# A hybrid attention and linear-attention block on one core: PSUM banks dealt out anew, half of one step's probabilities left in 32 bits, and who stores the linear-attention outputs

## The reference, cut to what matters

```
def blocked_attention(q, k, v):            # 8 query heads, 2 key/value heads, head size 64
    s = einsum('bqhgd,bkhd->bhgqk', q * Dh ** -0.5, k)      # latent: 2048 + 256 keys
    p = softmax(s, axis=-1)
    return einsum('bhgqk,bkhd->bqhgd', p, v)

def gla_chunked(q, k, v, g, s0):           # 4 heads, chunks of 64 tokens, forwards and backwards
    a = where(tril, einsum('bnihd,bnjhd->bnhij', q_t, k_t), 0)
    o_intra = einsum('bnhij,bnjhv->bnihv', a, v)
    o_inter = einsum('bnihd,bnhdv->bnihv', q_t, s_prev)
    ...
o_gla = rms_norm(o_f + o_b[:, ::-1], gla_g) * silu(og)
out = concatenate([o_gla, o_att], axis=-1) @ w_out
```

## Time and profile before

| | |
|---|---|
| median of three runs | 3334.68 us |
| the profiled execution | 3334.31 us |
| its span in the profile | 3332.5 us |
| PE busy, weight loads busy | 95%, 83% |
| DVE, ACT, POOL busy | 71%, 51%, 52% |
| attention | about 256 to 1064 us |
| GLA outputs | about 1488 to 1607 us |

### The profile page before, as it was taken

How to read it: one execution, slowest core, us unless ns; L and a number is a source line. 1 busy time by engine, 2 the same in 40 slices (tenths; PEclk the granted TensorE clock), 3 DMA queues, 4 the chain that set the end, 5 groups by cost and what they waited for, 6 DMA issues and landing times. The chain is left out here.

```text
span 3332.5 us, 48435 instructions
## 1 busy us (share of the span) xinstructions
PE 3163.3 (95%) x18066; PEld 2767.8 (83%) x18066; DVE 2377.7 (71%) x3263; ACT 1712.5 (51%) x2475; POOL 1718.4 (52%) x918
## 2 busy tenths in 40 slices
PE   6999999999997999998899799999999999999998
PEld 5986777777775997878688699999999999788886
DVE  4888999999996774349533688889888887223367
ACT  5867888888887784211344444443443333211122
POOL 2658999999997111101023377767766774000001
PEclk8999999999998999999999899999999999999999
DMA  6432101111111344338566577757785775554576
GB/s 223 163 122 79 49 22 50 45 51 45 47 33 58 135 150 134 113 117 259 168 214 196 168 243 231 239 161 227 228 257 155 222 220 158 213 188 178 180 262 220
DMA packets 434297, 518.42 MB, mean 156 GB/s; under 512 B 39712, under 2 KB 325328, under 8 KB 434064
## 3 DMA queue, kind: packets, MB, share of 16 engines
q1 hardware_dynamic: 387600, 414.46, 39.1%
q10 hardware_dynamic: 43440, 91.07, 7.9%
q0 software_dynamic: 3024, 9.80, 0.7%
HBM read 341.62 MB, written 173.64 MB: 155 GB/s over the span
## 5 line engine op out<-in xcount | busy, mean ns | idle before, releaser
L867 POOL TENSOR_TENSOR att_tlo<-att_prob,att_thi 128x1024 fp32r<-128x1024 f32 x292 | 694.3, 2403 | 41.7 <-ACT att_thi L1024 40.9
L168 PE MATMUL fu_p<-fu_hhi,fu_whi 128*128 128x384 f32 x1848 | 620.2, 336 | 24.9 <-PEq L113 17.3
L170 PE MATMUL fu_p<-fu_hhi,fu_wlo 128*128 128x384 f32 x1848 | 619.1, 335 | 0.0
L169 PE MATMUL fu_p<-fu_hlo,fu_whi 128*128 128x384 f32 x1848 | 619.1, 335 | 0.0
L1019 ACT ACTIVATE att_prob<-att_p_s 128x512 f32<-128x512 f32 x584 | 340.2, 591 | 88.4 <-PE att_p_s L919 81.2
L168 PEld LDWEIGHTS fu_p<-fu_hhi,fu_whi 128*128 128x128 f32 x1848 | 348.2, 188 | 27.3 <-issue 17.7
L1051 DVE TENSOR_REDUCE att_mx<-att_p_r 128x1 f32<-128x512 f32 x496 | 331.0, 684 | 33.4 <-PE att_p_r L882 32.3
L169 PEld LDWEIGHTS fu_p<-fu_hlo,fu_whi 128*128 128x128 f32 x1848 | 348.4, 189 | 0.0
L170 PEld LDWEIGHTS fu_p<-fu_hhi,fu_wlo 128*128 128x128 f32 x1848 | 348.2, 188 | 0.0
L1024 ACT ACTIVATE att_thi<-att_prob 128x1024 fp32r<-128x1024 f32 x292 | 309.7, 1061 | 9.3
L1866 POOL TENSOR_TENSOR fu_wsum<-fu_ws 128x1024 f32<-128x1024 f32 x66 | 182.7, 2768 | 237.0 <-DMA fu_ws<-in_w_ffn_dram 174.7
(11 more groups left out here) (371 smaller groups left out, 8027.4 us busy)
## 6 DMA issues: line engine op xcount, KB each, us to landing
fu_ws<-in_w_ffn_dram SPq DMA_DIRECT2D x132, 512.0 KB, 8.4
gated_d<-fu_out SPq DMA_DIRECT2D x99, 448.0 KB, 5.9
fd_src<-gated_d SPq DMA_DIRECT2D x63, 704.0 KB, 4.1
second_d<-fu_hs ACTq DMA_DIRECT2D x77, 512.0 KB, 3.3
fu_hs<-in_w_ffn_dram ACTq DMA_DIRECT2D x121, 256.0 KB, 4.3
fd_second<-second_d SPq DMA_DIRECT2D x40, 512.0 KB, 5.8
fd_w<-second_d SPq DMA_DIRECT2D x37, 512.0 KB, 5.3
ga_h<-hT_d SPq DMA_DIRECT2D x36, 512.0 KB, 4.2
```

What stands on the lines that cost most here:

```text
L168: pe.matmul(out, ah, bh, start=first, stop=False)
L169: pe.matmul(out, ah, bl, start=False, stop=False)
L170: return pe.matmul(out, al, bh, start=False, stop=last)
L867: pool.tensor_tensor(tlo[:, sl, :], prob[:, sl, :], thi[:, sl, :].bitcast(F32), ALU.subtract).then_inc(s.lo, 1)
```

## The change

Four things change.

1. **Banks.** `p_r` has three banks, `p_o` one. An item now waits for the item three places earlier. The first values of a unit wait until DVE has read the unit before (`osum` of that unit, not of the one before it). To give this time, PE's order changes around the end of a unit: the last values (both halves) come early in their step, and the first values of the next unit come at the end of the next step.
2. **Modulation parameters.** Their half chunk goes into a `p_r` bank as an item of the ring; DVE adds the bias at the start of the next step.
3. **One half-step unsplit.** For the second half of step 6 of each latent unit ACT copies no `thi` and POOL makes no `tlo`; PE multiplies the values with `prob` itself, as 32-bit floats (fp32), in one matmul in place of two in fp32r.
4. **GLA outputs.** ACT stores the finished tile itself, after its copy. SP loads the keys first, and waits for them only until the keys' buffer is free (`af`, `abk`), then the queries. In the output projection ACT waits once for these stores.

```diff
+    EXACT = (6,)
-        p_r = [ph.ps("p_r0"), ph.ps("p_r1")]
+        p_r = [ph.ps(f"p_r{i}") for i in range(3)]
-        p_o = [ph.ps("p_o0"), ph.ps("p_o1")]
+        p_o = ph.ps("p_o")
+        def exact(b, j, i):
+            return b.nds > 1 and i == 1 and j in EXACT
+        def split_cols(b, j):
+            return slice(0, ROW if exact(b, j, 1) else 2 * ROW)
...
+                if chunk is not None and j == CHUNK_STEP:
+                    S.part = (chunk, self.item(s.mod, chunk[0] * 2 + (chunk[1] + 1)))
...
+                        cols = split_cols(e, j)
-                        pool.tensor_tensor(tlo[:, sl, :], prob[:, sl, :], thi[:, sl, :].bitcast(F32), ALU.subtract).then_inc(s.lo, 1)
+                        pool.tensor_tensor(tlo[:, sl, cols], prob[:, sl, cols], thi[:, sl, cols].bitcast(F32), ALU.subtract).then_inc(s.lo, 1)
...
-                                wait(pe, s.osum, b.n - 1)
+                                wait(pe, s.osum, b.n)
+                        if exact(b, j, i):
+                            last = pe.matmul(p_o[:, :], v.bitcast(F32), prob[:, sl, cols], start=False, stop=j == b.nds - 1)
...
+                    begins = S.val and S.val[1] == 0
+                    ends = S.val and not begins and S.val[1] == S.val[0].nds - 1
-                    if S.val:
+                    if S.val and not begins:
                         values(0)
+                    if ends:
+                        values(1)
                     if pieces:
                         piece(*pieces.pop(0))
                     if S.now:
                         scores(1)
+                    if begins:
+                        for p in pieces:
+                            piece(*p)
+                        values(0)
+                        values(1)
...
-            if T := U.at(5):
-                sp.wait_ge(s.et, t + 1)
-                sp.dma_start(g.mix_tile(tile_at(t))[:, 0:GH * P], mT[:, par, :]).then_inc(s.st[par], 16)
+                wait(sp, s.af, GH * (t - OUT_BUFS + 1))
+                wait(sp, s.abk, GH * (t - OUT_BUFS + 1))
+                sp.dma_start(kT[:, n], ...).then_inc(s.qk[n], 16)
                 wait(sp, s.o, t - OUT_BUFS + 1)
                 ...two loads of qp...
-                sp.dma_start(kT[:, n], ...).then_inc(s.qk[n], 16)
...
                 act.activation(mT[:, par, :], p_m[:, :], ACT.Copy).then_inc(s.et, 1)
+                act.wait_ge(s.et, t + 1)
+                act.dma_start(g.mix_tile(tile_at(t))[:, 0:GH * P], mT[:, par, :]).then_inc(s.st[par], 16)
```

More of the change, by code:

```diff
@@ L751, in __init__ @@
             def __init__(self):
-                self.chunk, self.slots, self.ahead = None, [None] * SLOTS_P, iter([])
-                self.index, self.fin, self.ready, self.out, self.store, self.summed, self.done, self.ring = 1, None, None, None, None, None, [None, None, None], [None, None]
+                self.chunk, self.part, self.slots, self.ahead = None, None, [None] * SLOTS_P, iter([])
+                self.index, self.fin, self.ready, self.out, self.store, self.summed, self.done, self.ring = 1, None, None, None, None, None, [None, None, None], [None] * len(p_r)
             def item(self, sem, count):
-                bank, before = self.index % 2, self.ring[0]
+                bank, before = self.index % len(p_r), self.ring[0]
                 self.index += 1
-                self.ring = [self.ring[1], (sem, count)]
+                self.ring = self.ring[1:] + [(sem, count)]
                 return p_r[bank], before
@@ L792, in unit_steps @@
                     n = AHEAD if last else (PLAN if e.n else PLAN_FIRST)[j]
-                    S = self.step(e, j, v, n, v is not None and last, load if j == 0 else None)
-                    S.chunk = chunk
+                    S = self.step(e, j, v, n, v is not None and last, load if j == 0 else None, chunk)
                     yield S
@@ L931, in values @@
                         cols = slice(i * ROW, (i + 1) * ROW)
-                        pe.matmul(p_o[b.par][:, :], v, thi[:, sl, cols], start=j == 0 and i == 0, stop=False)
-                        last = pe.matmul(p_o[b.par][:, :], v, tlo[:, sl, cols], start=False, stop=j == b.nds - 1 and i == 1)
+                        if exact(b, j, i):
+                            last = pe.matmul(p_o[:, :], v.bitcast(F32), prob[:, sl, cols], start=False, stop=j == b.nds - 1)
+                        else:
+                            pe.matmul(p_o[:, :], v, thi[:, sl, cols], start=j == 0 and i == 0, stop=False)
+                            last = pe.matmul(p_o[:, :], v, tlo[:, sl, cols], start=False, stop=j == b.nds - 1 and i == 1)
                         if i == 1:
@@ L960, in step @@
                         scores(1)
-                    if len(pieces) > 1:
-                        piece(*pieces.pop(0))
-                    if S.val:
+                    if begins:
+                        for p in pieces:
+                            piece(*p)
+                        values(0)
                         values(1)
-                    for p in pieces:
-                        piece(*p)
-                    if S.chunk is not None and S.now[1] == CHUNK_STEP:
-                        (e, j), (c, half) = S.now, S.chunk
-                        wait(pe, s.osum, e.n)
+                    else:
+                        if len(pieces) > 1:
+                            piece(*pieces.pop(0))
+                        if S.val and not ends:
+                            values(1)
+                        for p in pieces:
+                            piece(*p)
+                    if S.part is not None:
+                        (c, half), (bank, before) = S.part
+                        if before:
+                            pe.wait_ge(*before)
                         pe.wait_ge(s.aw, c * 16 + 16)
@@ L975, in step @@
                                 col = half * HALF + q * QUART
[L976 removed]
+                                last = pe.matmul(bank[q * COLS:(q + 1) * COLS, 0:QUART], cpad[:, k, :], aw[:, k, col:col + QUART],
                                                  start=k == 0, stop=k == KC - 1)
@@ L1080, in step @@
                 def step(S):
+                    if S.sent is not None:
+                        (c, half), (bank, _) = S.sent
+                        dve.wait_ge(s.chunk, c * 2 + (half + 1))
+                        dve.wait_ge(s.adab, c * 32 + 32)
+                        dve.tensor_tensor(mod[:, half, :], bank[:, 0:QUART], adab[:, half, :], ALU.add).then_inc(s.mod, 1)
                     for p in S.early:
@@ L1111, in step @@
                         piece(*p)
-                    if S.chunk is not None and S.now[1] == CHUNK_STEP + 1:
-                        e, (c, half) = S.now[0], S.chunk
-                        dve.wait_ge(s.chunk, c * 2 + (half + 1))
-                        dve.wait_ge(s.adab, c * 32 + 32)
-                        dve.tensor_tensor(mod[:, half, :], p_o[1 - e.par][:, 0:QUART], adab[:, half, :], ALU.add).then_inc(s.mod, 1)
                 schedule(step)
@@ L2041, in step @@
                             act.wait_ge(s.table, 1)
+                            for n in range(2):
+                                act.wait_ge(g.op_st[n], 16 * (NT // 2))
                         act.wait_ge(s.tr, t + 1)
```

21 lines of the change are left out of this document (11 added, 10 removed).

## The result

The changed kernel takes **3362.56 us** (median of four runs, 3355.16 to 3365.59), the kernel before, on the same chip, 3334.70. The ratio is 1.0076 (95% interval 1.0062 to 1.0089): slower, as forecast, by 28 us where 12 were forecast. The time stands 1.6 us above the upper end of the range. The profiled execution took 3361.18 us, its span is 3359.4.

The account below looks back on a forecast made before the run. PE was taken to set attention's pace, POOL close behind, and DVE that of the GLA outputs. 3334.31 + 15 (attention) - 2.2 (GLA outputs) = 3347 us, slower; range for 8 in 10: 3318 to 3361.

Parts of the forecast that it names:

- the ring is late again: Rival, attention: ring costs 0.5 us per unit more and four context units stall twice; 3368 us, chance 0.10.
- PE sets the pace: Attention: PE, busy 789 of 808 us, is the limit; POOL, at 772, is close behind.
- Three ring banks: Attention's maxima ring: 1.4 us per unit lost in waits becomes about 0.2 (bounds 0 and 0.7).
- One output bank: Attention, unit's end: PE waits 1.14 us for `osum` plus 0.10 restart, 1.24 per unit (bounds 0.6 and 1.6).
- There is no slack elsewhere: Attention: nothing else in PE's unit absorbs the 1.24 us stall for the single output bank.
- Half a step in fp32: Latent units: one 0.88 us fp32 matmul replaces two 0.233 slots, +0.41 per unit on PE; POOL's relief buys nothing.
- Modulation in the ring: Units with a half chunk: same 1.1 us on PE, its bank free; zero, within 0.1.
- the walk: Attention: following DVE beside PE through the steps, PE finds its ring bank free by 0.3 to 1.3 us.
- Sum for attention: Units without a chunk 24.35 against 23.98, with one 25.35 against 24.78; 32 x 0.46 = +15 us.
- Context units at nothing: Attention's context units: no added cost, as ACT reads their values out before PE ends the next step's list.
- GLA outputs: GLA outputs: earlier query loads remove PE's load waits, -2.2 us (bounds 0 and -4); DVE's 5.85 per tile stays.
- The rival "the terms cancel": Attention: stall near 0.85, no other wait left, +0.07 to +0.16 per unit; 3336 us, chance 0.15.

Follow-up runs that it names:

- Run 3: Kernel before with the unsplit fp32 half step alone, banks and order as before: 3347.32 us, ratio 1.0031.
- run 6: Changed kernel with ACT's copy of the outputs (`osb`) moved one step earlier, ahead of the second exponential and `thi`: 3315.14 us, ratio 0.9931.
- run 10: Run 6 with two ring banks for the maxima instead of three: 3349.20 us, ratio 1.0038.
- run 7: Run 6 without the unsplit half step, all steps split in two rounded pieces: 3317.48 us, ratio 0.9938.
- Run 8: Changed kernel with the last maxima piece before a unit's first values computed five times, filling the wait for `osum`: 3347.08 us, ratio 1.0027.
- run 4: Changed kernel with two ring banks for the maxima instead of three, the eighth bank idle: 3407.62 us, ratio 1.0209.
- run 5: Run 4 with four matmuls into the idle bank ahead of each unit's first values: 3412.09 us, ratio 1.0228.
- run 2: Changed kernel without the unsplit fp32 half step, all steps split in two rounded pieces: 3334.06 us, ratio 0.9994.
- run 9: Changed kernel with one scores matmul more per unit, far from the wait for `osum`: 3366.51 us, ratio 1.0087.

## Why the prediction was right, and what it missed

The direction was forecast rightly and for the right reason; the size was not: 28 us came where 12 were forecast. The time alone is nearer to the rival "the ring is late again" (3368) than to the forecast (3347), but that mechanism did not occur: PE's weight loads wait 7.6 us for reductions, where it was 40.3 before. Step by step, in the prediction's order:

- **PE sets the pace.** Right. POOL waits 103.8 us for `thi`. By weight loads (600 of 808 us in the kernel before) POOL (772) would be the fuller engine. The Trainium skill's rule in "Perfetto Trace Analysis", Identifying the Most-Contended Engine, judges TensorE by FLOP utilization or by weight-load time, and by the second it would point to POOL; the first was not worked out here. Run 3 contradicts the second: 1.18 us less for POOL and 0.40 more for PE cost 0.39 a unit.
- **Three ring banks, -1.2 a unit.** 1.15 and 0.93, measured in runs 6 and 10 where nothing else differs.
- **One output bank, +1.24 a unit.** The wait is 1.09 and the loss 1.26 in the trace. Taking it away gives 24.25 - 23.03 = 1.22 in units without a chunk, but only 0.63 in those with one (25.45 - 24.82). "There is no slack elsewhere" was thus right for one kind of unit. The Trainium skill asks in "Perfetto Trace Analysis", Optimizing Tensor Performance, for matmul groups that rotate through PSUM banks; runs 6 and 10 say where that pays here: a third bank for the ring is worth some 35 us, while one output bank causes no wait in the middle of the stage once its read-out starts early.
- **Half a step in fp32, +0.41.** 0.39 to 0.40, in two pairs of kernels. Four times the 128-column row was a good scale. That the fp32 step buys nothing was right, and stays right without the stall (run 7).
- **Modulation in the ring, no wait.** Mis-sized: a chunk makes a unit 1.20 longer, forecast 1.00. The weight loads of L1000 wait 6.5 us for reductions, 16 times, so the bank was not free as the walk had it.
- **Sum for attention.** Units that keep the clock: 24.25 and 25.45, forecast 24.35 and 25.35. The two errors of 0.10 cancel, which is luck: 16 x (0.27 + 0.67) = 15.0 us, forecast 15. The forecast also took all 32 units for such units. Only 26 distances are; they give 12.1 us, and the first two and the tail give 0.8 back. So without the falls the stage grows by 11.3 us from the first `qb` copy to the last, not by 15. Run 8, where the clock is kept, confirms the smaller sum: +8.9 us by its ratio, where 12.5 were forecast (11.3, and 2.5 at the end of the stage, less 5 in the GLA outputs, is 8.8). That its time of 3347.08 is the forecast's 3347 is chance, since the kernel before took 3338.23 in its group.
- **Context units at nothing.** Their last wait of 2.1 us and the fall behind it cost about 2.5 us.
- **GLA outputs, -2.2.** Mis-sized: -5.3, known within about 3. The direction and the two waits in the middle were right; the last four tiles give 3 us more.
- **What is missing: TensorE's clock.** The prediction valued a wait of 1.1 us at its length. In 11 of 31 cases it also left the matmuls behind it at half speed, 17 us in the latent units alone, more than the 11 us of all the rest. Nothing in the rows read before spoke of it: the ring's waits were short (0.17 us in the earlier trace rows, 0.34 on average in the earlier trace rows), and the clock stood at 1.00 in the pair of units. This term alone carried the time past the range, which had been made from the stall's and the fp32 matmul's bounds.
- **The rival "the terms cancel".** Its sum is off. With 0.85 for the stall and no other wait, a unit without a chunk is 22.9 + 0.85 = 23.75, 0.23 less than before, and only the one with a chunk is longer (0.07 to 0.17). That gives some 3330, not 3336; both count as "same".

On the cause: it is shown that the falls stand behind the waits for `osum` or, in runs 4 and 5, with the ring's wait at the same place; that they go when the wait is filled with matmuls (run 8) or removed (run 6); that the fp32 matmul is not needed (run 2); and that equal units with equal waits fall or don't (run 9). Because one equal wait in several has a fall, the absence of falls in one kernel could be chance. Over the changed kernel and runs 2 and 9, 19 of 81 waits of 1.09 us have one behind them (nine, one and nine); of the 27 filled waits of run 8 none has, and in the middle of run 6's stage there is neither a wait for `osum` nor a fall. From run 9 it follows that the moment plays a part. In the changed kernel a fall lengthens the pair of units from 49.70 to 51.23 us, and the nine falls ahead of the tail come 51.2 us apart; that the pair's new length keeps them in step is my reading, and no run varied it on its own. Why the falls of run 2 stopped after the first is open in the same way.

The two profiles add up: span +26.9 us; first `qb` copy +2.3 (ahead of attention, where the program is the same; over all the traces here this copy starts between 254.4 and 257.3 us, so it belongs to the execution and not to the change); to the last copy +28.3, of which 17 are the falls; then about +2.5 at the very end of attention, where the 2.1 us wait and the eleventh fall lie; -4.9 to the output projection; the rest, -1.3, is spread behind it.

## What to carry to other kernels

When a change adds a wait to TensorE in a stretch that was dense, price it twice: once as long as it is, once with the clock that may fall behind it, here 1.5 us behind one in three of the waits of 1.1. Before a bank is taken away, look at what stands ahead of its read-out in the list of the engine that reads it: one ScalarE copy moved ahead of two instructions turned +28 us into -23. And if a wait can't be avoided, work in it can be faster than idling: here even repeated matmuls were (run 8); useful ones were not tried.

## What was not expected of the hardware

- A wait of 1.09 us on TensorE can halve its granted clock for 3.38 us (1.2 in place of 2.4 GHz; matmuls of 128x512 start 0.42 us apart instead of 0.233). Of 27 such waits of the changed kernel nine had a fall behind them; of the 27 filled waits of run 8, 0.18 us long, none.
- One more matmul per unit changed which units were hit, and four more matmuls per unit, in the wait, made the kernel 16 us faster by the two ratios (run 8).
- An fp32 matmul of 512 columns holds TensorE for 0.87 us, 3.7 times one in fp32r (0.233 us).
